# Modulation with the weight tiles stationary, the gate summed on VectorE inside the merge, and the low-rank part taken k by k

## What is computed

```python
shift_c, scale_c, gate_c = _modulation(c_ctx, w_mod[l], b_mod[l])
h_ctx = _rmsnorm(ctx, norm_g[l]) * (1.0 + scale_c) + shift_c
...
shift, scale, gate = _modulation(c, w_mod[l], b_mod[l])
h = _rmsnorm(x, norm_g[l]) * (1.0 + scale[:, None]) + shift[:, None]
y, _ = _mix(_features(h, lp, grid=True), lp, ctx_states, emit=True)
x = x + gate[:, None] * y.astype(x.dtype)
```

## Time and profile before

| | |
|---|---|
| median of 3 runs | 2841.43 us (2834.56 to 2842.79) |
| the profiled execution | 2840.47 us |
| its span, first to last instruction | 2838.7 us |
| PE busy | 2644.4 us, 93% |
| PEld busy | 2349.8 us, 83% |
| POOL busy | 1411.9 us, 50% |
| ACT busy | 1110.8 us, 39% |
| DVE busy | 1042.6 us, 37% |
| mean granted clock of PE | 0.962 |

### The profile page before, as it was taken

How to read it: one execution, slowest core, us unless ns; L and a number is a source line. 1 busy time by engine, 2 the same in 40 slices (tenths; PEclk the granted TensorE clock), 3 DMA queues, 4 the chain that set the end, 5 groups by cost and what they waited for, 6 DMA issues and landing times.

```text
span 2838.7 us, 66948 instructions
## 1 busy us (share of the span) xinstructions
PE 2644.4 (93%) x27478; PEld 2349.8 (83%) x27478; DVE 1042.6 (37%) x1668; ACT 1110.8 (39%) x1658; POOL 1411.9 (50%) x621
## 2 busy tenths in 40 slices
PE   7998899999999879998999997998989999999998
PEld 5675677777777767777999997998889989999997
DVE  0205667666766713332111104333323033323311
ACT  0103234333443433333444435454444355455443
POOL 0006221122212214444888884776667867777785
PEclk9998799999999969999999998999999999999999
DMA  8682111111111102223555551444444534444453
GB/s 304 224 286 88 53 61 34 49 49 61 47 43 49 47 26 89 91 86 131 192 182 180 185 182 60 159 163 148 141 140 152 190 115 150 160 164 148 162 179 118
DMA packets 97975, 361.28 MB, mean 127 GB/s; under 512 B 10880, under 2 KB 12032, under 8 KB 97440
## 3 DMA queue, kind: packets, MB, share of 16 engines
q1 hardware_dynamic: 96624, 354.95, 37.7%
q10 hardware_dynamic: 1200, 4.04, 0.4%
HBM read 356.85 MB, written 2.10 MB: 126 GB/s over the span
## 4 chain that ended last, share of the span: by engine, by line
PE 81%; issue 6%; DVE 5%; ACT 4%; POOL 3%; DMA 0%; SPq 0%; ACTq 0%; DVEq 0%; POOLq 0%
PE ps L193 16%; PE ps L195 15%; PE ps L194 15%; PE ps L312 5%; PE ps L493 5%; POOL wlo L181 3%; PE ps L494 3%; PE ps L495 3%; PE ps L579 2%; PE ps L643 2%; ACT whi L171 2%; PE ps L664 1%; PE ps L1698 1%; DVE W L353 1%; PE ps L713 1%
## 5 line engine op out<-in xcount | busy, mean ns | idle before, releaser
L181 POOL TENSOR_TENSOR wlo<-raw,whi 128x1024 fp32r<-128x1024 f32 x566 | 1363.2, 2427 | 1350.3 <-ACT whi L171 1322.4
L193 PE MATMUL ps<-ahi,whi 128*128 128x256 f32 (+1 forms) x3760 | 1120.1, 298 | 63.4 <-POOL wlo L181 31.0
L194 PE MATMUL ps<-alo,whi 128*128 128x256 f32 (+1 forms) x3760 | 1100.8, 293 | 0.0
L195 PE MATMUL ps<-ahi,wlo 128*128 128x256 f32 (+1 forms) x3760 | 1099.9, 293 | 0.0
L193 PEld LDWEIGHTS ps<-ahi,whi 128*128 128x128 f32 x3760 | 728.7, 194 | 98.0 <-POOL wlo L181 39.2
L171 ACT ACTIVATE whi<-raw 128x1024 fp32r<-128x1024 f32 x566 | 584.8, 1053 | 433.5 <-PE ps L195 257.8
L195 PEld LDWEIGHTS ps<-ahi,wlo 128*128 128x128 f32 x3760 | 730.5, 194 | 10.3
L194 PEld LDWEIGHTS ps<-alo,whi 128*128 128x128 f32 x3760 | 731.0, 194 | 9.7
L493 PE MATMUL ps<-ahi,whi 128*128 128x256 f32 (+1 forms) x512 | 208.7, 408 | 3.3 <-ACT W L843 2.9
L312 PE MATMUL ps<-raw,small 128*2 128x128 f32 x1536 | 173.8, 276 | 21.2 <-DMA raw<-stream 14.0
L312 PEld LDWEIGHTS ps<-raw,small 128*2 128x2 f32 x1536 | 130.9, 86 | 64.3 <-DMA raw<-stream 14.6
(11 more groups left out here) (301 smaller groups left out, 2981.4 us busy)
## 6 DMA issues: line engine op xcount, KB each, us to landing
raw<-stream SPq DMA_DIRECT2D x662, 512.0 KB, 3.3
W<-xT SPq DMA_DIRECT2D x1, 4096.0 KB, 17.6
XR<-xT ACTq DMA_DIRECT2D x1, 2048.0 KB, 7.4
outT<-XR SPq DMA_DIRECT2D x4, 512.0 KB, 2.7
cns<-consts SPq DMA_DIRECT2D x1, 1120.0 KB, 5.4
cns<-consts ACTq DMA_DIRECT2D x1, 896.0 KB, 9.6
W<-pair_par ACTq DMA_DIRECT2D x6, 146.0 KB, 2.2
W<-pair_par SPq DMA_DIRECT2D x2, 146.0 KB, 4.0
```

Source lines behind the costliest of these rows:

```text
L181: nc.gpsimd.tensor_tensor(wlo[slot], raw[slot], whi[slot].bitcast(F32), ALU.subtract).then_inc(lo_done, 1)
L193: nc.tensor.matmul(out, whi[slot][:, k, :], mh, start=first and k == 0, stop=False)
L194: nc.tensor.matmul(out, whi[slot][:, k, :], ml, start=False, stop=False)
L195: ins = nc.tensor.matmul(out, wlo[slot][:, k, :], mh, start=False, stop=last and k == UK - 1)
```

## The change

- **Modulation.** Only shift and scale are computed at the start: 64 units. Now the 128 x 128 block is the stationary operand and the conditioning pair (128 x 2) the moving one, so the result lands on 128 partitions, and the copies and transposes are gone. The sum-of-squares matmuls are no longer one block; one stands behind every second unit, from output tile 8 to 23, with four `sq` buffers.
- **Scaled input.** ACT writes `ahi` directly from the normed input with scale and bias. DVE computes `hf` as before and, one k later, `alo`. POOL only splits weights. ACT's first four splits are put between its first k's.
- **Low-rank part.** k by k: for each k nine matmuls, three for each output tile. The six units are reordered on the host; PE waits for three split units at a time, and a unit is free only after the eighth k of its half.
- **Gate.** Its 32 units go to the end of the stream (`GATE`). In the merge SP loads two of them per output tile into `graw0` and `graw1`, behind a wait until the previous tile's sum is done. DVE sums `weight block x condition` over the 16 blocks in a chain of 16 dependent operations on `gacc`; PE sums `gacc` over the partitions with a one-column matmul; DVE adds the bias.

```diff
-U_MOD = 96
+U_MOD = 64
...
             for k in range(KT):
                 nc.vector.tensor_tensor(xin[:, :, k, :], xin[:, :, k, :], r3, ALU.mult).then_inc(s_xn, 1)
...
+        def pe_norm(pe, k):
+
+            pe.wait_ge(s_sq, k + 1)
+            nc.tensor.matmul(ps[:, 7, :], meanw, sq[:, k % 4], start=k == 0, stop=k == KT - 1).then_inc(s_sqmm, 1)
         def pe_mod(pe):
             pe.wait_ge(s_pre, 1)
...
+            for n in range(2 * KT):
+                for u in range(2):
+                    m = 2 * n + u
+                    pe.wait_ge(raw_in[m % RING], (m // RING + 1) * 16)
+                    for k in range(UK):
+                        ins = nc.tensor.matmul(ps[:, 0, 2 * n:2 * n + 2], raw[m % RING][:, k, :], scond[:, UK * u + k, :],
+                                               start=u == 0 and k == 0, stop=u == 1 and k == UK - 1)
+                    ins.then_inc(mod_used, 1)
+                if 8 <= n < 8 + KT:
+                    pe_norm(pe, n - 8)
         def dve_mod(dve):
...
             dve_norm(dve)
...
+            dve.wait_ge(mod_used, U_MOD)
             bias = pv[:, PV["b_mod"]].unsqueeze(2).broadcast_to([P, 48, 2])
...
+            rows = ps[:, 0, 0:4 * KT].rearrange("p (n c) -> p n c", c=2)
+            nc.vector.tensor_tensor(mod_v[:, 0:2 * KT, :], rows, bias[:, 0:2 * KT, :], ALU.add).then_inc(s_mod, 1)
             dve.wait_ge(s_mod, 1)
             g = pv[:, PV["norm_g"]].unsqueeze(2).broadcast_to([P, KT, 2])
             nc.vector.scalar_tensor_tensor(gm_v, mod_v[:, KT:2 * KT, :], 1.0, g, ALU.add, ALU.mult).then_inc(s_mod, 1)
             dve.wait_ge(s_mod, 2)
             dve.wait_ge(s_xn, KT)
+            for k in range(KT + 1):
+                if k < KT:
+                    if k >= 4:
+                        dve.wait_ge(s_hlo, k - 3)
+                    for s in range(2):
+                        nc.vector.tensor_scalar(hf[:, k % 4, s], xin[:, s, k, :], gm_v[:, k, s:s + 1],
+                                                mod_v[:, k, s:s + 1], ALU.mult, ALU.add).then_inc(s_h, 1)
+                if k:
+                    dve.wait_ge(s_h, 2 * k)
+                    dve.wait_ge(s_hhi, 2 * k)
+                    nc.vector.tensor_tensor(alo[:, :, k - 1, :], hf[:, (k - 1) % 4], ahi[:, :, k - 1, :].bitcast(F32),
+                                            ALU.subtract).then_inc(s_hlo, 1)
+
+        def act_h(act):
+            act.wait_ge(s_mod, 2)
             for k in range(KT):
...
+                act.wait_ge(s_xn, k + 1)
                 for s in range(2):
...
+                    nc.scalar.activation(ahi[:, s, k, :], xin[:, s, k, :], ACT.Identity, bias=mod_v[:, k, s:s + 1],
+                                         scale=gm_v[:, k, s:s + 1]).then_inc(s_hhi, 1)
+                if 1 <= k <= 3:
+                    split_hi(act, k - 1, k - 1)
+                elif k == 8:
+                    split_hi(act, 3, 3)
         def pool_h(pool):
             for s in range(RING):
                 split_lo(pool, s, s)
...
         s_lora = sem("s_lora")
         s_lcp = sem("s_lcp")
         def pe_lora(pe):
...
+            for u in range(2):
+                pe.wait_ge(lo_done, 3 * u + 3)
+                for k in range(UK):
+                    kt = UK * u + k
+                    pe.wait_ge(s_hlo, kt + 1)
+                    for t in range(3):
+                        slot = (3 * u + t) % RING
+                        out = ps[:, 2 + t, :]
+                        nc.tensor.matmul(out, whi[slot][:, k, :], ahi[:, :, kt, :], start=kt == 0, stop=False)
+                        nc.tensor.matmul(out, whi[slot][:, k, :], alo[:, :, kt, :], start=False, stop=False)
+                        ins = nc.tensor.matmul(out, wlo[slot][:, k, :], ahi[:, :, kt, :], start=False, stop=kt == KT - 1)
+                        if k == UK - 1:
+                            ins.then_inc(unit_used, 1)
         def act_lora(act):
             for s in range(RING, U_LORA + LEAD):
                 split_hi(act, s % RING, s)
...
+            act.wait_ge(unit_used, 6)
             nc.scalar.activation(LWA[:, 0, :], ps[:, 2, :], ACT.Tanh).then_inc(s_lcp, 1)
...
             nc.scalar.activation(LWA[:, 1, :], ps[:, 3, :], ACT.Copy).then_inc(s_lcp, 1)
...
             nc.scalar.activation(LG[:, :], ps[0:32, 4, :], ACT.Copy).then_inc(s_lcp, 1)
         def pool_lora(pool):
...
                     mm_tile(pe, b, i, 12, 0, ps[:, bank, 0:T], 0)
                     mm_tile(pe, b, i, 12, 2, ps[:, bank + 1, 0:T], 0)
                     M["ylo"].wait(pe, 4)
+                    M["gate_ok"].wait(pe, i * 2 + n)
                     for u in range(2):
                         mm_unit(pe, (b + 4 + u) % RING, i * 12 + (b + 4 + u), ps[:, bank + 2 + u, 0:T], 1, UK * u, True,
                                 True)
+                    M["gate_acc"].wait(pe, (i * 2 + n + 1) * KT)
+                    nc.tensor.matmul(ps[:, 6 - bank, T:T + 1], gacc[:, :], kst_[:, 2:3], start=True, stop=True)\
+                        .then_inc(M["gate_mm"].sem, 1)
         def act_merge(act):
             with act.Fori(0, KT // 2) as i:
...
                 for k in range(RING):
                     split_lo(pool, (base + k + LEAD) % RING, (i, RING, base + k + LEAD))
+        def sp_merge(sp):
+
+            with sp.Fori(0, KT // 2) as i:
+                for r in range(2 * U_MERGE):
+                    sp.wait_ge(lo_done, i * (2 * U_MERGE) + (S_MERGE + r - RING + 1))
+                    load_unit(sp, (S_MERGE + r) % RING, i * (2 * U_MERGE) + (U_MOD + S_MERGE + r))
+                    n, r6 = r // U_MERGE, r % U_MERGE
+                    if r6 in (2, 3):
+                        u = r6 - 2
+                        M["ylo"].wait(sp, 4)
+                        M["gate_acc"].wait(sp, (i * 2 + n) * KT)
+                        sp.dma_start(graw[u].rearrange("p k n -> p (k n)"),
+                                     stream[bass.ds(i * 4 + (GATE + 2 * n + u), 1)].rearrange("a p n -> (a p) n"))\
+                            .then_inc(M[f"gate_in{u}"].sem, 16)
+
         def dve_merge(dve):
             with dve.Fori(0, KT // 2) as i:
                 for n in range(2):
+                    for kt in range(KT):
+                        tile, ck = graw[kt // UK][:, kt % UK, :], scond[:, kt, 0:1]
+                        if kt % UK == 0:
+                            M[f"gate_in{kt // UK}"].wait(dve, (i * 2 + n + 1) * 16)
+                        if kt == 0:
+                            nc.vector.tensor_scalar(gacc[:, :], tile, ck, None, ALU.mult).then_inc(M["gate_acc"].sem, 1)
+                        else:
+                            M["gate_acc"].wait(dve, (i * 2 + n) * KT + kt)
+                            nc.vector.scalar_tensor_tensor(gacc[:, :], tile, ck, gacc[:, :], ALU.mult, ALU.add)\
+                                .then_inc(M["gate_acc"].sem, 1)
                     M["tg"].wait(dve, i * 4 + 2 * n + 2)
                     dve.wait_ge(unit_used, i * 12 + (S_MERGE + U_MERGE * n + 6))
                     for g in range(2):
...
                     nc.vector.tensor_tensor(mlo[:, nsl, :].rearrange("p a t -> p (a t)"), mx[:, n, :],
                                             mhi[:, nsl, :].rearrange("p a t -> p (a t)").bitcast(F32), ALU.subtract)\
                         .then_inc(M["mlo"].sem, 1)
+                    M["gate_mm"].wait(dve, i * 2 + n + 1)
+                    gsl = bass.ds(2 * i + (2 * KT + n), 1)
+                    nc.vector.tensor_tensor(mod[:, :].rearrange("p (n c) -> p n c", c=2)[:, gsl, 0],
+                                            ps[:, 6 - 4 * n, T:T + 1], pv[:, PV["b_mod"]][:, gsl], ALU.add)\
+                        .then_inc(M["gate_ok"].sem, 1)
         def out_phase(name, base, gate, hi_, lo_, sel, ready):
...
             sp_mod(sp)
             sp_stream(sp)
             sp_pairs(sp)
-            sp_loop(sp, S_GLA, S_END - S_GLA)
+            sp_loop(sp, S_GLA, S_MERGE - S_GLA)
+            sp_merge(sp)
+            sp_loop(sp, S_OUT1, S_END - S_OUT1)
             sp_store(sp)
         @block.gpsimd
```

More of the change, by code:

```diff
@@ L47 @@
 S_END = S_OUT3 + U_OUT * KT
+GATE = U_MOD + S_END
 PV = {}
@@ L294, in dve_norm @@
                 nc.vector.tensor_tensor(xin[:, :, k, :], xin[:, :, k, :], r3, ALU.mult).then_inc(s_xn, 1)
-        def pe_norm(pe):
-            for k in range(KT):
-                pe.wait_ge(s_sq, k + 1)
-                nc.tensor.matmul(ps[:, 7, :], meanw, sq[:, k % 2], start=k == 0, stop=k == KT - 1).then_inc(s_sqmm, 1)
-        def mod_rounds(pe, first, end):
-            with pe.Fori(first, end) as i:
-                for g in range(2):
-                    if g == 0:
-                        modcp.wait(pe, i * 2)
-                    for t in range(2):
-                        for u in range(2):
-                            r = 2 * t + u
-                            pe.wait_ge(raw_in[r], (i * 2 + g) * 16 + 16)
-                            for k in range(UK):
```

(7 more changed lines are left out.)

62 lines of the change are left out of this document (13 added, 49 removed).

## The result

The changed kernel takes 2986.6 us (median of 4 runs, 2985.3 to 2988.6), the kernel before, beside it, 2842.1 us (2834.6 to 2849.5): a ratio of 1.0509, 95% interval 1.0481 to 1.0538. The forecast was 2972. The profiled execution took 2985.31 us with a span of 2983.5, against 2838.7 before; the 144.8 us between the two spans are what follows is about.

A forecast was written before the change was run, and what follows sets the result against it. The prediction took PE to bound the kernel almost everywhere. Its terms, 48.5 (modulation) + 2.7 + 1.5 (scaled input, low-rank part) + 79 (gate in the merge) = 131.7 us, gave 2972 us, range 2848 to 3010 at about eight in ten.

The forecast's parts named there:

- The clock in the modulation: Modulation on PE: the two-column matmuls were taken to run at half clock, 1.2 GHz, throughout, as the earlier transposes did.
- The size of it: Modulation: 0.222 us an instruction, 3.55 us a unit, plus 27 us for the sum of squares, ending at 263.
- term 1: Modulation: inputs can be scaled from 263.5 us, where before it was 215.0, so +48.5 us.
- Scaled input and low-rank part: Between modulation and pairs: PE starts the low-rank part later, +2.7 us, and that part takes longer, +1.5 us.
- The price of a link: Gate chain on DVE: 0.38 us a link alone, about 2.5 under POOL's splits, one operation through per split.
- The tile: Merge: DVE's gate chain makes a tile 22.0 us against 17.28, PE idling 4 to 5; sixteen tiles, 75 us.
- The start of the merge: Start of the merge: SP waits for the split of y before loading the fourth unit, 4 us, once.
- The stages that the change doesn't touch: Pairs and linear attention, and all behind the merge: forecast to change by 0 us.
- A: Rival on the modulation: it runs at full clock or its loads don't slow down, 2855 us; chance 0.20.
- C: Rival, faster: full clock in the head outweighs what the merge's tiles lose, 2784 us at the lower bound; chance 0.06.
- B: Rival on the merge: half clock in the modulation, but the gate's chain hides, 2901 us; chance 0.09.
- D: Rival: the change doesn't do what it says, e.g. a starved raw ring, tile over 25 us, over 3015 us; chance 0.03.

The follow-up runs named there:

- wide64: The changed kernel with 64 moving columns instead of 2 in the modulation (the conditioning pair repeated): 2903.5 us, ratio 1.0197 to the kernel before.
- wide128: The changed kernel with 128 moving columns instead of 2 in the modulation (the conditioning pair repeated): 2877.2 us, ratio 1.0121 to the kernel before.
- gate_alone: The kernel before with only the gate moved to the merge; old modulation form, scaled input and low-rank order: 2879.4 us, ratio 1.0123.
- acc_psum: The changed kernel with the accumulator of the gate's chain in PSUM instead of SBUF: 2915.4 us, ratio 1.024 to the kernel before.
- gate_at_start: The changed kernel with the gate's 32 units back in the modulation, in the new form, and the old merge: 3007.6 us, ratio 1.0553 to the kernel before.
- gate_on_act: The changed kernel with wide128's and acc_psum's edits, the gate loads issued from ScalarE's queue and SP's loop as before: 2803.7 us, ratio 0.9854.
- best: The changed kernel with wide128's and acc_psum's edits and the gate loads issued behind a tile's raw loads: 2800.4 us, ratio 0.986 to the kernel before.

## Why the forecast was nearly right, step by step

**The clock in the modulation: right.** All of the stage ran at 1.2 GHz. The forecast took the transposes of the earlier trace rows for the pattern of the stage. That row was thin evidence, since PE also stood idle when the level fell; it is wide64 and wide128 that bear the step out: with the same loads and more moving columns the pace doubles. What would have shown it was named wrongly: PEclk says 1.00 there. The durations have to be read. The kernel before had the same trap in its first 12.6 us, where L312's instructions came at half the pace of the earlier trace rows under a PEclk of 1.00.

**The size of it: 0.222 us was 0.213.** That is 60 x 0.14 = 8 us too much, all of the miss of term 1. The sum of squares was 16 x 1.70 = 27 us, as forecast. The end is 22.95 + 60 x 3.41 + 27.3 = 254.9, and the trace has 255.2. The 0.222 was twice the 0.111 of the earlier trace rows. In wide64 and wide128 the same load goes from 0.213 to 0.111 us with the level of the clock, a factor of 1.92 and not 2. (The upper bound that the forecast gave, 1.11 / 4, is 0.28 and not 0.27; it would have moved the term by 53 us and not 46.) "TensorE: Matmul & The Clock Gate" of the Trainium skill, section "LDWEIGHTS (loading the stationary operand)", gives a load's time as its columns over 1.2, in ns, with no word of the clock. By it 128 columns take 107 ns (an estimate from that page): that agrees with the upper level here and is off by two at the lower one.

**Scaled input and low-rank part: right to 2 us.** PE waited 4.6 us in the middle where 5.9 was forecast, and at the end the two splits and the table load stood before the evictions as described. gate_alone has neither part of the change and loses nothing by it.

**The price of a link: right.** 0.38 us free, 2.4 us under a split, one link for each split. The Trainium skill, "SBUF — State Buffer", section "SBUF: two separate sides", says that VectorE and GpSimd share a pair of ports as an exclusive lock held for a whole instruction, which a VectorE operation needs if it has two SBUF inputs and the GpSimd one reads SBUF; acc_psum agrees, where a link with one SBUF and one PSUM input takes 0.39 us under a running split.

**The tile: 22.0 forecast, 21.8 measured, and by the mechanism forecast.** DVE's chain sets the tile. In the tile from 1485.93 DVE starts 3.6 us behind the last chain's end, ten links go free and six are held, as forecast; one of the six is held for 1.67 us only, and 0.97 us is a wait for the second unit, which landed 6.0 us after its issue (the first took 3.3, as assumed). What was wrong is PE's side of it: its idle time is 2.6 us a tile, not 4 to 5, because its matmuls run 2.0 us longer behind the waits. The tiles at the full clock are no more than 0.2 us shorter on average, so this mostly filled idle time. Whoever counts only PE's waits, 39 us, still sees less than half of what the gate costs; gate_at_start gives back all of it.

**The start of the merge: 8.7 us forecast, 13.0 measured.** The 13.0 us are what the merge has gained (82.3) without the 15 tiles behind the first (69.3). They hold the first tile's own chain, so the forecast's 4 us and its 4.7 for one tile stand beside them. The step left out what ACT's queue issues when y is split: 2.9 MB for XR and the constants, the first of it 0.3 us ahead of the loads that SP had held back. DMA issues between 1387 and 1405 us (count, KB each, median us to landing):

```profile
XR<-xT ACTq DMA_DIRECT2D x1, 2048.0 KB, 8.4
raw<-stream SPq DMA_DIRECT2D x4, 512.0 KB, 13.0
graw<-stream SPq DMA_DIRECT2D x2, 512.0 KB, 10.6
```

13.0 us to landing where the earlier trace rows has 3.3; PE waited 10.7 us for POOL. From the last split of y to the first mixed tile it is 31.9 us here, 30.0 in acc_psum and 22.0 in gate_on_act, with SP freed of the wait; but there the second mixed tile came 4 us later behind the first than in best, since the first gate unit was late in its turn. That the 2.9 MB delay the loads is argued from the order of issue; no run moved them.

**The stages that the change doesn't touch: 0 forecast, +19 us between the two profiles.** This was the largest miss. The forecast's 131.7 us against 144.8 are 19 too few here and 3 in the merge, less 8 too many in the modulation and 1 in the two stretches behind it. The misses run both ways, so that the sum is 13 us off where its parts are 31 off: some luck is in it. PE is busy longer with the same instructions: 996.6 against 986.7 us in pairs and linear attention, 1151.9 against 1144.7 behind the merge; it is so by the clock (0.93 against 0.94 in the first of them). The clock falls at other gaps of the pairs than before. How much of the 19 us belongs to the change is open: the kernel before alone took 2831.4 to 2851.3 us in the seven executions beside gate_at_start, at granted clocks of 0.967 to 0.958, and single profiles can't say in which stage that lies. Why all ten kernels with a part of the change lie above both profiles of the kernel before is open too. The new low-rank part and the new modulation aren't needed for it, as gate_alone has the old ones and took 1074.7 us; it may be the time at which a stage begins or the place of the code, and neither was tried alone.

**The rivals.** A and C needed the upper level without more columns; B needed links that pass a split, which only another operand gave; D needed a tile over 25 us, which was 21.8. C, "faster", is what best became, by changing the two things on which the forecast rested.

## What to carry to other kernels

When an operand is made stationary and little moves, ask first at what clock the engine will run: repeating the moving columns up to what a load hides was free here, and took the end of this stage from 255 to 148 us. Work for VectorE that is to run beside GpSimd should read one of its two tensors from PSUM; the accumulator is a good one to put there. Take the price of a new wait from the length of the whole stage, not from the waits of the engine that is fed: here they were 39 of 88 us. And loads that were held back meet whatever else was let go by the same event.

## What the runs showed of the hardware that was not expected

- PE can be busy without a gap for 232 us (22.95 to 255.2) and stay at the lower level: the two-column matmuls did, with a 512-column step behind every second unit of the middle. In wide64 it stayed low for 74 us, rose among the 512-column matmuls and was still high through the last 256 instructions, the same as at the start. In wide128 it rose 5.5 us after the start, with no other matmul before it.
- The granted clock of these profiles reads 1.00 until the first recorded change, whatever the level is (shown by the paces up to 271 us in the changed kernel, up to 12.6 in the one before).
- A link that reads one tensor from PSUM and writes SBUF isn't held by a split of POOL: 0.35 us against 2.4. Having one tensor in SBUF and none in PSUM isn't enough. Timeline of DVE, then POOL, in the scaled input of the changed kernel:

```profile
268.86 2.47 DVE L329 TENSOR_SCALAR W<-W,gmul,mod 128x256 f32<-128x256 f32 x1
...
268.56 2.62 POOL L182 TENSOR_TENSOR wlo<-raw,whi 128x1024 fp32r<-128x1024 f32 x1 [2.67 <-ACT whi L172]
```

Alone, four of these take 1.38 us; beside the split one takes 2.47. "SBUF — State Buffer" of the Trainium skill, section "Who interferes with whom", counts `tensor_scalar` among the operations that can enter a 2-port mode and then contend with GpSimd; the 2.47 us agree, though no run shows the mode itself.
